# Forgetting attention taken two heads at a time, with the bias products of a pair on two halves of TensorE's rows

## The reference

```python
def fox_mixer(h, w_in, b_forget, w_out):
    q, k, v, gate, f = split_cols(h @ w_in, ODD_SPLITS)
    qh = heads(q) * FOX_HEAD_DIM ** -0.5
    log_f = jax.nn.log_sigmoid(f + b_forget)
    cum = jnp.cumsum(log_f, axis=1).transpose(0, 2, 1)
    # per block of 128 queries, for every head
    s = jnp.einsum('bhqd,bhkd->bhqk', qb, kh) + cb[..., :, None] - cum[:, :, None, :]
    a = jax.nn.softmax(jnp.where(causal_mask(start, T), s, NEG_INF), axis=-1)
    o = jnp.einsum('bhqk,bhkd->bhqd', a, vh)
    ...
    o = o * jax.nn.sigmoid(gate)
    return o @ w_out
```

## Times and profile before

| | us |
|---|---|
| median of three runs | 3607.71 |
| lowest and highest of them | 3601.76 and 3613.13 |
| the profiled execution | 3595.51 |
| its span on the core | 3593.7 |
| TensorE busy in it | 3265.5 (91%) |
| VectorE busy | 2034.7 (57%) |
| ScalarE busy | 1299.3 (36%) |

### The profile page before, as it was taken

One profiled execution on the slowest core, in us unless ns is written; L12 is line 12 of the kernel. 1 busy time (PEld: TensorE's weight loads), 2 busy tenths in 40 slices (PEclk: granted clock), 3 DMA queues, 4 the chain that ended last, 5 costly groups with the idle time before them and its releaser, 6 DMA issues.

```text
span 3593.7 us, 51778 instructions
## 1 busy us (share of the span) xinstructions
PE 3265.5 (91%) x21422; PEld 2599.9 (72%) x21422; DVE 2034.7 (57%) x3609; ACT 1299.3 (36%) x2143; POOL 375.4 (10%) x334
## 2 busy tenths in 40 slices
PE   6898899999898999998996888879999889989998
PEld 4667778887685688886765666567777677768886
DVE  5445467754433476755545437688778763554444
ACT  3234242222323342223432135465555533333321
POOL 0001100000000000000001000055445420000000
PEclk9898899999998999999997989999999989999999
DMA  3220034432230134432220120211111103223231
GB/s 128 62 71 1 16 103 141 141 129 88 75 101 24 53 112 146 141 112 77 94 71 18 48 94 25 68 53 41 45 39 38 51 5 106 82 95 104 94 96 68
DMA packets 297352, 274.77 MB, mean 76 GB/s; under 512 B 10400, under 2 KB 287008, under 8 KB 296352
## 3 DMA queue, kind: packets, MB, share of 16 engines
q1 hardware_dynamic: 292864, 256.07, 22.3%
q10 hardware_dynamic: 4256, 15.40, 1.2%
HBM read 265.16 MB, written 6.29 MB: 76 GB/s over the span
## 4 chain that ended last, share of the span: by engine, by line
PE 80%; DVE 10%; ACT 5%; issue 3%; POOL 1%; DMA 0%; DVEq 0%; ACTq 0%; SPq 0%; POOLq 0%
PE ps L95 79%; DVE f L107 3%; DVE f L101 2%; DVE r L101 2%; PE ps L98 2%; ACT f L88 1%; ACT f L92 1%; ACT r L92 1%; POOL f L101 1%; DVE f L104 1%; ACT f L89 1%; DVE f L113 1%; ACT L88 1%; DVE f L110 1%; DVE r L107 0%
## 5 line engine op out<-in xcount | busy, mean ns | idle before, releaser
L95 PE MATMUL ps<-r,r 128*128 128x512 f32 x10368 | 2443.8, 395 | 110.6 <-DVE r L101 71.4
L95 PEld LDWEIGHTS ps<-r,r 128*128 128x128 f32 x10368 | 1933.4, 191 | 565.3 <-issue 140.2
L95 PE MATMUL ps<-f,f 64*64 64x64 f32 (+9 forms) x10116 | 769.5, 267 | 173.7 <-ACT f L92 45.8
L101 DVE TENSOR_TENSOR r<-f,r 128x1024 fp32r<-128x1024 f32 (+2 forms) x621 | 656.1, 1063 | 433.4 <-ACT r L92 427.9
L95 PEld LDWEIGHTS ps<-f,f 64*64 64x64 f32 (+3 forms) x10116 | 586.9, 157 | 344.1 <-issue 162.4
L92 ACT ACTIVATE r<-f 128x1024 fp32r<-128x1024 f32 (+2 forms) x548 | 506.7, 937 | 764.3 <-PE ps L95 649.7
L101 POOL TENSOR_TENSOR f<-f,f 128x256 f32<-128x256 f32 (+1 forms) x276 | 332.3, 1217 | 472.6 <-ACT f L88 263.7
L107 DVE SCALAR_TENSOR_TENSOR f<-f,f,f 128x128 f32<-128x128 f32 (+3 forms) x622 | 365.5, 593 | 26.4 <-ACT f L88 7.3
L101 DVE TENSOR_TENSOR f<-ps,f 128x512 f32<-128x512 f32 (+7 forms) x333 | 180.3, 554 | 336.0 <-PE ps L95 326.6
L92 ACT ACTIVATE f<-ps 128x256 f32<-128x256 f32 (+3 forms) x422 | 183.4, 451 | 514.3 <-PE ps L95 366.4
L88 ACT ACTIVATE f<-ps 128x512 f32<-128x512 f32 (+3 forms) x203 | 111.9, 553 | 586.6 <-PE ps L95 584.6
(11 more groups left out here) (33 smaller groups left out, 733.8 us busy)
## 6 DMA issues: line engine op xcount, KB each, us to landing
f<-in_w_mlp_up SPq DMA_DIRECT2D x32, 1024.0 KB, 6.0
f<-in_w_mlp_down SPq DMA_DIRECT2D x32, 1024.0 KB, 6.3
f<-in_w_ff SPq DMA_DIRECT2D x32, 1024.0 KB, 5.1
f<-in_w_ada SPq DMA_DIRECT2D x48, 512.0 KB, 3.9
f<-in_w_in SPq DMA_DIRECT2D x24, 1024.0 KB, 5.1
f<-in_w_in SPq DMA_DIRECT2D x44, 512.0 KB, 3.6
f<-in_w_in_even SPq DMA_DIRECT2D x12, 1024.0 KB, 5.2
f<-in_w_in_odd SPq DMA_DIRECT2D x12, 1024.0 KB, 5.2
```

What stands on the lines that cost most here:

```text
L95: return self.e.matmul(out, l, r, start=first, stop=last)
L101: return self.e.tensor_tensor(out, a, b, op)
```

## The change

Units are taken in another order: two heads a pair, and for each block of queries both heads before the next block. In the even unit of each two TensorE does the bias products of both heads one behind the other, the first from rows 0 to 39 and the second from rows 64 to 103 of `L` and `rh`, into two banks, and behind them the two full products onto them. In the odd unit no scores are left to do. The tiles get the second set of rows: `lf` has four copies of the heads, `fox.cum` 104 columns, VectorE makes four copies out of PSUM and writes both `rh` of a pair at its first unit.

```diff
--- before.py
+++ after.py
@@ -23,8 +23,8 @@
      "gdn_gc": 4, "gdn_kdf": 4, "gdn_DTm": 4, "gdn_Kb": 4, "gdn_Qd": 4, "gdn_KBE": 4, "gdn_VB": 4, "gdn_AT": 12, "gdn_QKT": 4,
      "gdn_x0": 2, "gdn_xt0": 18, "gdn_x1": 2, "gdn_xt1": 18, "gdn_VN": 4, "gdn_S": 17, "gdn_DTu": 4, "gdn_al0": 12,
      "gdn_al1": 12, "gdn_z": 2, "ev_o": 4, "ev_hg": 4, "ev_hd": 4, "ev_lg": 4, "ev_ld": 4, "ev_zs": 4},
-    {"fox_fr": 1, "fox_f": 1, "fox_q": 8, "fox_k": 8, "fox_va": 4, "fox_vd": 4, "fox_g": 8, "fox_y": 2, "fox_zero": 5,
-     "fox_lf": 2, "fox_cum": 2},
+    {"fox_fr": 1, "fox_f": 1, "fox_q": 8, "fox_k": 8, "fox_va": 4, "fox_vd": 4, "fox_g": 8, "fox_y": 2, "fox_zero": 7,
+     "fox_lf": 4, "fox_cum": 4},
     {"fox_exp": 32, "fox_pt": 32, "fox_row": 8, "fox_max": 32, "fox_r": 32, "fox_n": 32, "fox_out": 8},
     {"mem_v": 2, "mem_q": 4, "mem_g": 4, "mem_exp": 16, "mem_pt": 16, "mem_k": 4, "mem_max": 16, "mem_den": 16, "mem_sn": 16,
      "mem_out": 4},
@@ -395,7 +395,7 @@
     z = np.zeros((128, 8))
     for j in range(8):
         z[j, j] = 1.0
-        z[32 + j, j] = 1.0
+        z[32 + j, j] = z[64 + j, j] = z[96 + j, j] = 1.0
     c["one40"] = z
     c["pad"] = np.zeros((128, HEAD - 256 - sum(c[k].shape[1] for k in ("eps", "invf1", "invf2", "eps5", "epsg", "one40"))))
     m = np.zeros((128, 512))
@@ -2060,7 +2060,7 @@
         self.f = al(4, 8)
         self.y, self.sp_ = al(32), al(32)
         self.e, self.w, self.l = al(32), al(32), al(32)
-        self.lf = al(4, 40)
+        self.lf = al(4, 104)
         self.L, self.Rb = al(T), al(T)
         self.rh = [al(T) for _ in range(2)]
         self.sc, self.pt = [al(T) for _ in range(4)], [al(T) for _ in range(3)]
@@ -2068,7 +2068,7 @@
         self.o = K.h
         self.X = Split(K, lambda j: K.hh_r[:, j, :], lambda j: K.h_r[:, j, :])
         self.out = OutProj(K, "odd.out", K.A["w_out_odd"][0], self.X, x_done)
-        self.units = [(h, qt) for h in range(8) for qt in range(4)]
+        self.units = [(2 * a + b, qt) for a in range(4) for qt in range(4) for b in range(2)]
         self.bank = {}
 
     def pe(self, pe):
@@ -2085,21 +2085,27 @@
         G.lin_tm(pe, "fox.v", W, 2048, 1024, X, lambda tt, b: [("fox_v" + "da"[tt % 2], 2 * b + tt // 2 + 1)])
         for n in range(8):
             G.tile(pe, ("fox.g", n), W, 3072 + n * 128, 128, X, [("fox_g", n + 1)])
-        pe.wait_ge("fox_lf", 2)
-        b = self.bank["cum"] = K.ps.take(pe, ("fox_cum", 2))
+        pe.wait_ge("fox_lf", 4)
+        b = self.bank["cum"] = K.ps.take(pe, ("fox_cum", 4))
         ub = K.c("ubig")
         for j in range(4):
-            t = pe.mm(K.ps.t[b][0:40, :], self.lf[:, j, :], ub[:, 384 - 128 * j:896 - 128 * j], j == 0, j == 3)
+            t = pe.mm(K.ps.t[b][0:104, :], self.lf[:, j, :], ub[:, 384 - 128 * j:896 - 128 * j], j == 0, j == 3)
         K.mm_done(t, "fox.cum")
         pe.fence()
         for u, p in waves(32, 6):
             h, qt = self.units[u]
             km, qs = (qt + 1) * 128, slice(qt * 128, qt * 128 + 128)
             if p == 0:
-                pe.wait_ge("fox_row", h + 1)
-                b = self.bank["s", u] = K.ps.take(pe, ("fox_max", u + 1))
-                pe.mm(K.ps.t[b][:, 0:km], self.q[:, h, qs], self.k[:, h, 0:km], True, False)
-                K.mm_done(pe.mm(K.ps.t[b][:, 0:km], self.L[0:40, qs], self.rh[h % 2][0:40, 0:km], False, True), ("fox.s", u))
+                if h % 2:
+                    continue
+                pe.wait_ge("fox_row", h + 2)
+                for w in range(2):
+                    r = slice(64 * w, 64 * w + 40)
+                    b = self.bank["s", u + w] = K.ps.take(pe, ("fox_max", u + w + 1))
+                    pe.mm(K.ps.t[b][:, 0:km], self.L[r, qs], self.rh[w][r, 0:km], True, False)
+                for w in range(2):
+                    b = self.bank["s", u + w]
+                    K.mm_done(pe.mm(K.ps.t[b][:, 0:km], self.q[:, h + w, qs], self.k[:, h + w, 0:km], False, True), ("fox.s", u + w))
             elif p == 3:
                 pe.wait_ge("fox_n", u + 1)
                 b = self.bank["t", u] = K.ps.take(pe, ("fox_pt", u + 1))
@@ -2197,23 +2203,26 @@
         dve.settle()
         dve.wait_ge("fox_zero", 1)
         s3 = blocks(self.sp_, 4)
-        for o in (0, 32):
+        for o in (0, 32, 64, 96):
             dve.ts(self.lf[:, :, o:o + 8], s3, -1.0, None, MUL, None).then_inc(S("fox_lf"), 1)
         dve.wait_ge("mm", K.done["fox.cum"])
-        dve.wait_ge("fox_zero", 5)
+        dve.wait_ge("fox_zero", 7)
         p = K.ps.t[self.bank["cum"]]
-        dve.cp(self.L[32:40, :], p[32:40, :]).then_inc(S("fox_cum"), 1)
-        dve.cp(self.Rb[0:8, :], p[0:8, :]).then_inc(S("fox_cum"), 1)
+        for o in (0, 64):
+            dve.cp(self.L[o + 32:o + 40, :], p[o + 32:o + 40, :]).then_inc(S("fox_cum"), 1)
+            dve.cp(self.Rb[o:o + 8, :], p[o:o + 8, :]).then_inc(S("fox_cum"), 1)
         dve.fence()
         mask, one = K.c("mask"), K.c("one40")
         for u, p in turns(32, (0, 1, 2, 5)):
             h, qt = self.units[u]
             km, qs = (qt + 1) * 128, slice(qt * 128, qt * 128 + 128)
             sc, col = self.sc[u % 4], self.col[u % 6]
-            if p == 0 and qt == 0:
-                if h >= 2:
-                    dve.wait_ge("mm", K.done["fox.s", 4 * (h - 2) + 3])
-                dve.ts(self.rh[h % 2][0:40, :], self.Rb[0:40, :], one[0:40, h:h + 1], None, MUL, None).then_inc(S("fox_row"), 1)
+            if p == 0 and qt == 0 and h % 2 == 0:
+                for w in range(2):
+                    r = slice(64 * w, 64 * w + 40)
+                    if h:
+                        dve.wait_ge("mm", K.done["fox.s", u - 2 + w])
+                    dve.ts(self.rh[w][r, :], self.Rb[r, :], one[r, h + w:h + w + 1], None, MUL, None).then_inc(S("fox_row"), 1)
             elif p == 1:
                 dve.wait_ge("mm", K.done["fox.s", u])
                 if u >= 4:
@@ -2237,11 +2246,13 @@
         K, S = self.K, self.K.S
         self.norm.gps(pool)
         pool.memset(self.lf, 0.0).then_inc(S("fox_zero"), 1)
-        pool.memset(self.L[0:32, :], 0.0).then_inc(S("fox_zero"), 1)
-        pool.wait_ge("fox_zero", 2)
-        pool.memset(self.L[0:8, :], -1.0).then_inc(S("fox_zero"), 1)
-        pool.memset(self.Rb[0:32, :], 0.0).then_inc(S("fox_zero"), 1)
-        pool.memset(self.Rb[32:40, :], 1.0).then_inc(S("fox_zero"), 1)
+        pool.memset(self.L[0:96, :], 0.0).then_inc(S("fox_zero"), 1)
+        pool.memset(self.Rb[0:96, :], 0.0).then_inc(S("fox_zero"), 1)
+        pool.wait_ge("fox_zero", 3)
+        for o in (32, 96):
+            pool.memset(self.Rb[o:o + 8, :], 1.0).then_inc(S("fox_zero"), 1)
+        for o in (0, 64):
+            pool.memset(self.L[o:o + 8, :], -1.0).then_inc(S("fox_zero"), 1)
         pool.fence()
         for j in range(8):
             if self.X.on_pool(j):
```

## The result

| | before | after |
|---|---|---|
| median of four runs, us | 3608.93 (3601.76 to 3613.13) | 3586.43 (3583.94 to 3594.78) |
| ratio, 95% interval | | 0.9941 (0.992 to 0.9962) |
| profiled execution, us | 3595.51 | 3583.94 |
| span, us | 3593.7 | 3582.1 |

The changed kernel is faster by 0.6%, 22 us where 6.3 were forecast, and its time lies under the range. A second comparison with nine runs against 31 gave 0.9964 (0.9948 to 0.9979), so 13 us (7.6 to 18.7); one further run of before, at 8132 us, is left out of it.

A forecast was written before the change was run, and what follows sets the result against it. TensorE was taken as the bound, with one wait per head. Loop -8.4 us and +2.1 us ahead of it gave -6.3: 3607.7 (profiled execution carried to the median) to 3601.4 us, range 3590 to 3612.

The forecast's parts named there:

- the steady pair: Loop at 2.4 GHz: a pair of heads takes 1.85 us less than its 19.8 us.
- overlap: Loop: bias products side by side on two row halves cost one, 2.15 us less per pair of heads.
- the old wait: End of each head: TensorE's wait for ScalarE's copy behind an exponential of 512 columns goes, 1.40 us less per pair.
- the row count's changes: Loop: two changes between 128 and 40 rows per two units, not four, at 0.20 us each; 1.60 us less per pair.
- The four waits: Odd units: no scores cover ScalarE's copy, so TensorE waits four times a pair; 3.3 us more (2.6 to 4.5).
- Rival 3: Loop: more waits, TensorE about 82% busy, keep the clock low or drop it; up to 3646 us; chance 0.08.
- rival 1: Loop's bias products overlap only in the middle passes or not at all; 3605.7 or 3610.0 us; chance 0.10.
- what goes ahead of the loop: Before the loop: more writes of `lf`, copies of 8 rows and one more `rh`; 2.1 us more.
- the slow part: Loop's first 20 us at 1.2 GHz: concurrent passes save there once more; 1.0 us less (0 to 4).
- rival 2: Loop's start: denser products raise the clock 10 us sooner, gaining some 5 us, to 3596; chance 0.15.
- same execution: Whole kernel: before's profiled execution of 3595.5 us would take 3589.2 with the change, 6.3 us less.
- Rival 4: Loop's end falls otherwise against the clock's drop at 1208.20; time moves by 3.4 us, within each case's range.

The follow-up runs named there:

- same order, no overlap: The changed kernel with both bias products of a pair on rows 0 to 39, so they can't run side by side; 0.999 to before, 20.12 us a pair.
- copy moved: The kernel before with only ScalarE's copy of the transposed probabilities put ahead of the round's exponential; 0.9992 to before, two heads 18.41 us.
- in turn: The changed kernel with the second bias product behind the first full one (bias, full, bias, full); 1.0021 to before, 21.57 us a pair.
- delayed before: The kernel before with three more VectorE instructions ahead of the loop, so that it starts some 1.9 us later; 1.0021 to before, loop 100.2 us.
- after_late: The changed kernel with two more VectorE copies ahead of the loop, which starts 1.4 us later; 0.9983 to before, median 3594.8 us.
- the next step: The kernel before with bias products over all 128 rows, and ScalarE's copy also put ahead of its exponential; 0.9927 to before, median 3580.02 us.

## Why the prediction was wrong

Its direction was right, and so was each price in the steady state; the size failed at one term, and by what lies outside of the edited part.

**Right: the steady pair.** 17.95 us were worked out, 17.98 measured. The parts are shown apart: overlap 2.15 forecast, 2.14 measured (same order, no overlap); the old wait 1.40 and 1.40 (copy moved); the row count's changes 1.60 and 1.45 (in turn); the same arithmetic gave the other kernels' two heads to 0.15 us. The four waits showed 0.37, 0.58, 0.58 and 0.69 us of idle time; with the 0.27 that the earlier trace rows had between idle time and lost time that is the 3.3 us of the sum. (Rival 3's 82% mixes the two: by idle time TensorE was busy 15.78 of 18.00 us, 88%, beside before's 94%.) Two products on two halves cost one, so rival 1 is out. The Trainium skill (TensorE: Matmul & The Clock Gate, section "The mechanism") has matmuls start and end in program order. Read pass by pass, as the prediction read it, the trace disagrees: a pair of 512 columns takes 1.06 us and not 1.49, and two passes start together twice. Read product by product it agrees, since the second product neither starts nor ends ahead of the first.

**Right: what goes ahead of the loop.** +2.1 forecast, +2.4 and +2.1 measured in the two pairs of traces.

**Failed: "I take 1.0 us more saved (0 to 4)" for the slow part, loop -8.4.** The loop is 11.8 and 12.0 us shorter. Four pairs at 1.83 are 7.3 of it; the other 4.5 to 4.7, past the 0 to 4 of the term, are the clock. The time at 0.50 in the loop is 11.5 and not 20.4 us, 8.9 less, and a microsecond's work at 0.50 that is done at 1.00 gives back half. Of the 8.9, 6.8 are the shorter stretch, 1.8 the loop's later start in it, and 0.4 the drop at the end. I had held the 20 us fixed and only doubled the passes in it. That was rival 2, with a chance of 0.15; its guess of 5 us was the measured size. Shown is that the stretch goes with the loop's own instructions: at one starting place it is 13.7 us with paired and 20.5 with separate bias products, and at another it is 17.1 to 20.5 with products of 40 rows and 3.4 without. The starting place counts too (27.3 in the delayed before, 10.2 in the delayed after). By which of their properties the clock is set isn't shown: the changes of row count and the share of rows in use go together here.

**Failed, in the "same execution" of the sum: that nothing else moves.** The sum ran against before's profiled execution, and all but the edited part was to stay. The rest got 6.7 us shorter with the same instructions and the part ahead 4.5 longer. Rival 4 saw the end of the loop alone (3.4 us; the drop at 1208.20 is indeed gone), not that the places behind it can swap too. Over the traces the rest is 2376.8 to 2386.8 us and the part ahead 1102.3 to 1119.5. The shorter rest came with the pairs' order in six traces, but 2.5 us more work ahead of it swapped it both ways, so it hangs on how the work falls against the clock, and the prediction's sum had no term for that.

**Beyond the sum: the step to the median.** The prediction added the 12.2 us between before's profiled execution and its median. Before's profiled execution stood 13 us under its median of four, after's 2.5 under its own. More than half of the 13 lies in the part ahead, in which nothing is edited: 1102.5 us in that trace, where the middle of all sixteen is 1110. From the forecast to the measured 3586.4 are 15.0 us: 9.7 of them this step, 3.4 the loop, 2.2 the unchanged parts together (6.7 - 4.5), less 0.3 for the head. As far as the runs show, the 9.7 are the draw of few executions: before's median was 3602 to 3608 us in the five later comparisons, beside 3608.9 in the first.

**Open.** The traces explain 9.4 to 9.9 us by the edited part, which lies within the second comparison's 7.6 to 18.7, but below the first one's (14 to 29). For the second one the clocks of the timed runs divide the difference, by the estimate used for the moved copy: the means differ by 12.1 us, 7.5 of them (5.5 to 9.5) not of the clock, and after stood 9 us less at 0.50 (22 less to 3 more), which is worth half. The loop alone has 8.9 us less at 0.50. With the rest's 16.4 less, and 1.8 more ahead of the loop, it would be some 23, so the timed runs give no support for a gain behind the loop; for the first comparison before's clocks aren't on record, and its larger difference stays open. So does after_late's 0.9983 beside after's 0.9964: without the clock's cost it is 7.3 us under before, as after is, and the time at 0.50 scatters too much between runs to tell 1.4 us.

## What to carry to other kernels

Price the steady state from rows of the same form elsewhere in the trace; here that was good to 0.03 us in 18. Hold no stretch of the granted clock fixed when the instructions in it change, and give the unchanged parts a spread of their own (here 10 us behind the edit and 17 ahead of it). Where each run's mean clock is on record, compare span times clock too: that told 6 us where the time told none. And before two small products are set side by side, try the plain form over all rows: it needed a handful of changed lines, gave about what the pairing gave (0.9939 beside 0.9941 and 0.9964), and left the order free for the next step (0.9927).

## What the runs showed of the hardware

A product over 40 of 128 rows between full ones was dearer than one over all 128, of which 88 are zeros: two heads took 19.81 us with it and 17.86 without. The Trainium skill (TensorEngine Tiling (Array Packing), section "Key Properties") says that a change of the tiling mode drains TensorE. The trace fits it, with some 0.20 us at each change of the row count and no load issued ahead there; that it is a drain no row shows.

With TensorE idle ahead of the loop, the slow stretch at the loop's start was 3.4 us without products of 40 rows, and 10.2 to 27.3 us with them. A start 1.9 us later came with 8 us more in the loop of before, one 1.4 us later with 2 us less in that of after (one trace each).

Float32 products on two row halves, 512 columns: two records start at 1154.41 and two at 1154.95, and the pair takes 1.06 us; on one half it takes 1.91.

An unchanged part of 2380 us took 2376.8 to 2386.8 us, with 224 to 252 us at 0.50, and one of 1110 us took 1102.3 to 1119.5, with 106 to 143.
